# Three-pass products that walk the moved columns and their bank's columns from the last to the first

## What is computed

```python
def _swiglu(h, w13, w2):
    gte, up = jnp.split(h @ w13, 2, axis=-1)
    return (jax.nn.silu(gte) * up) @ w2

def peer_ffn(h, w_pq, sub_keys, expert_u, expert_v):
    ...
        u = jnp.take(expert_u, ic, axis=0)
        a = jnp.einsum('cd,chkd->chk', hc, u)
        w = gc * jax.nn.gelu(a, approximate=False)
        return jnp.einsum('chk,chkd->cd', w, jnp.take(expert_v, ic, axis=0))
```

## Time and profile before

| | us |
|---|---|
| median of 3 runs | 3823.09 |
| lowest and highest | 3820.19, 3826.91 |
| the profiled execution, its span | 3825.9 |
| TensorE busy in it | 3753.4 |
| VectorE, ScalarE, GpSimd busy | 2803.7, 1752.2, 576.4 |

### The profile page before, as it was taken

The page is one execution under the profiler, slowest core; times in us unless marked ns, Lnnn a source line. Parts: engine busy times, 40 slices in busy tenths (PEclk is TensorE's granted clock), DMA queues, the critical chain, the costliest instruction groups (busy, mean ns, idle before and its releaser), DMA issues.

```text
span 3825.9 us, 68450 instructions
## 1 busy us (share of the span) xinstructions
PE 3753.4 (98%) x22768; PEld 3354.5 (88%) x22768; DVE 2803.7 (73%) x4900; ACT 1752.2 (46%) x2723; POOL 576.4 (15%) x244
## 2 busy tenths in 40 slices
PE   8999999999999999999999999999999999999998
PEld 7888888888888879998999999888888999997886
DVE  7867777776863556654588888888644688888888
ACT  3223323223322354445546776333465557774334
POOL 0000000000000000055675000000356770000000
PEclk9999999999999999999999999999999999999999
DMA  6544434454542324563456666777634466666775
GB/s 252 177 158 156 158 132 153 145 181 138 176 138 85 97 67 153 181 209 117 142 180 224 208 206 202 241 242 240 228 126 145 155 228 207 209 212 220 241 241 197
DMA packets 203862, 685.43 MB, mean 179 GB/s; under 512 B 22560, under 2 KB 24864, under 8 KB 194336
## 3 DMA queue, kind: packets, MB, share of 16 engines
q1 hardware_dynamic: 174880, 573.45, 46.2%
q10 hardware_dynamic: 28800, 109.59, 7.8%
HBM read 646.25 MB, written 36.70 MB: 179 GB/s over the span
## 4 chain that ended last, share of the span: by engine, by line
PE 81%; POOL 8%; issue 7%; DVE 2%; DMA 1%; ACT 1%; POOLq 0%; SPq 0%; DVEq 0%; ACTq 0%
PE bank L584 25%; PE bank L586 25%; PE bank L585 25%; POOL low L544 8%; PE bank L1152 2%; PE bank L626 1%; PE bank L680 0%; PE bank L681 0%; PE bank L685 0%; PE bank L791 0%; DMA x<-in_x 0%; DVE low L1684 0%; PE bank L769 0%; PE bank L836 0%; DVE h L1663 0%
## 5 line engine op out<-in xcount | busy, mean ns | idle before, releaser
L1228 ACT ACTIVATE high<-raw 128x1024 fp32r<-128x1024 f32 x1044 | 1098.9, 1058 | 1288.8 <-PE bank L586 987.8
L584 PE MATMUL bank<-h_lo,high 128*128 128x256 f32 (+1 forms) x4080 | 1280.5, 314 | 7.0 <-ACT h_hi L1627 3.6
L586 PE MATMUL bank<-h_hi,low 128*128 128x256 f32 (+1 forms) x4080 | 1276.5, 313 | 0.0
L585 PE MATMUL bank<-h_hi,high 128*128 128x256 f32 (+1 forms) x4080 | 1274.4, 312 | 0.0
L1684 DVE TENSOR_TENSOR low<-raw,high 128x1024 fp32r<-128x1024 f32 x808 | 971.4, 1219 | 79.3 <-ACT high L1228 77.2
L544 POOL TENSOR_TENSOR low<-raw,high 128x1024 fp32r<-128x1024 f32 x240 | 576.2, 2407 | 2571.7 <-DVE low L1684 2325.3
L584 PEld LDWEIGHTS bank<-h_lo,high 128*128 128x128 f32 x4080 | 772.2, 189 | 56.6 <-DVE h_lo L1759 4.9
L585 PEld LDWEIGHTS bank<-h_hi,high 128*128 128x128 f32 x4080 | 772.2, 189 | 47.3 <-issue 0.7
L586 PEld LDWEIGHTS bank<-h_hi,low 128*128 128x128 f32 x4080 | 771.6, 189 | 46.5
L584 PE MATMUL bank<-low,weighed_hi 128*128 128x512 f32 x1024 | 401.1, 392 | 8.5 <-DVE weighed_lo L1684 8.5
L585 PE MATMUL bank<-high,weighed_hi 128*128 128x512 f32 x1024 | 400.7, 391 | 0.0
(11 more groups left out here) (319 smaller groups left out, 4825.6 us busy)
## 6 DMA issues: line engine op xcount, KB each, us to landing
raw<-in_experts SPq DMA_DIRECT2D x516, 512.0 KB, 3.5
raw<-in_w SPq DMA_DIRECT2D x176, 512.0 KB, 4.2
late_raw<-in_mod_late ACTq DMA_DIRECT2D x64, 1024.0 KB, 4.8
acts_spill<-acts_out ACTq DMA_DIRECT2D x128, 256.0 KB, 3.8
acts_in<-acts_spill SPq DMA_DIRECT2D x128, 256.0 KB, 3.4
raw<-in_w_in SPq DMA_DIRECT2D x56, 512.0 KB, 3.4
raw<-in_w SPq DMA_DIRECT2D x64, 384.0 KB, 3.1
raw<-in_w SPq DMA_DIRECT2D x64, 320.0 KB, 3.6
```

The costliest lines, as they stand in the source:

```text
L584: pe.matmul(out, a[0], b[1], start=start, stop=False, **more)
L585: pe.matmul(out, a[0], b[0], start=False, stop=False, **more)
L586: return pe.matmul(out, a[1], b[0], start=False, stop=stop, **more)
L1228: act.activation(high[:, slot * UNIT:(slot + 1) * UNIT], raw[:, slot * UNIT:(slot + 1) * UNIT], ACT.Copy)\
```

## The change

A helper `falling` reverses the columns of the views it is given. `product3` uses it for its bank and for both parts of the moved operand; the stationary operand is as before. `project_first` does the same for its own matmuls. Every matmul of these products thus reads its moved columns from the last to the first and writes the bank's columns from the last to the first, and each sum ends in the column where it was.

```diff
--- before.py
+++ after.py
@@ -579,8 +579,13 @@
                 pe.wait_ge(S["low_ready"], unit.next())
                 return [part[:, slot * UNIT:(slot + 1) * UNIT] for part in (high, low)]
 
+            def falling(*parts):
+
+                return [part[:, ::-1] for part in parts]
+
             def product3(out, a, b, start, stop, **more):
 
+                out, *b = falling(out, *b)
                 pe.matmul(out, a[0], b[1], start=start, stop=False, **more)
                 pe.matmul(out, a[0], b[0], start=False, stop=False, **more)
                 return pe.matmul(out, a[1], b[0], start=False, stop=stop, **more)
@@ -670,26 +675,26 @@
                 w = [take() for _ in outs]
 
                 def parts(n, k):
-                    return [part[:, k * P:(k + 1) * P] for part in w[n]], rhs[n](k)
-
+                    return [part[:, k * P:(k + 1) * P] for part in w[n]], falling(*rhs[n](k))
+
+                down = falling(*outs)
                 for k in range(KD // 2):
 
                     wait("normed", per_tile)
                     for n in range(len(outs)):
                         a, b = parts(n, k)
-                        pe.matmul(outs[n], a[0], b[0], start=(k == 0), stop=False)
-                        pe.matmul(outs[n], a[1], b[0], start=False, stop=False)
+                        pe.matmul(down[n], a[0], b[0], start=(k == 0), stop=False)
+                        pe.matmul(down[n], a[1], b[0], start=False, stop=False)
                     wait("split")
                     for n in range(len(outs)):
                         a, b = parts(n, k)
-                        pe.matmul(outs[n], a[0], b[1], start=False, stop=False)
+                        pe.matmul(down[n], a[0], b[1], start=False, stop=False)
                 T["normed"].next(per_tile * (KD - KD // 2))
                 for n in range(len(outs)):
                     for k in range(KD // 2, KD):
                         if n == 0:
                             wait("split")
-                        a, b = parts(n, k)
-                        mm = product3(outs[n], a, b, False, k == KD - 1)
+                        mm = product3(outs[n], [part[:, k * P:(k + 1) * P] for part in w[n]], rhs[n](k), False, k == KD - 1)
                     mm.then_inc(unit_used, 1)
 
             def up_tiles(n, cols, fresh=False):
```

## The result

The changed kernel takes 3877.31 us (median of 4 runs, 3870.59 to 3880.55) against 3824.11 for the kernel before beside it (4 runs, 3820.19 to 3826.91). The ratio is 1.0144, with a 95% interval of 1.0131 to 1.0156: slower by 1.4%, where 1.2% faster was forecast. All ratios are over fast executions alone; the single slow one of the runs told of here, 5331.8 us with all moved tiles 16 columns ahead, is in none of them.

The account below looks back on a forecast made before the run. The prediction took TensorE's matmul pace to bound the kernel; savings of 13.3, 29.4 and 1.9 us sum to 44.6, giving a span of 3781.3 and, with the profiled span 2.8 us over the median, 3779 us; range 3640 to 3965.

Parts of the forecast that it names:

- What bounds the kernel: Whole kernel: as long as its matmuls are apart, TensorE busy 98% of the span; 20,688 of 22,768 matmuls touched.
- The paces of before: Distances between starts: 226.7 ns aligned and 233.3 with h2 stationary at 512 columns; 120.0 aligned and 116.7 with h2 moved at 256.
- What I take: Three-pass products: walks starting apart and crossing sooner give every backward matmul the 10.0 ns excess of h2 moved at 256.
- The terms: Savings by matmul group: 13.3 us from aligned 256s, 29.4 and 1.9 from 512s, 0 elsewhere; sum 44.6 us.
- That all of it reaches the end: Other engines keep up, VectorE at 18.5 of 20 us, so all 44.6 us shorten the span to 3781.3.
- Slower by crossings: Rival: opposed walks meet three times as often, 6.6 ns on each of 20,496 matmuls, 135 us, 3958; chance 0.15.
- The indifferent case: Rival: direction doesn't matter because the excess is a fixed swap of weights; 3823 within 8 us; chance 0.20.
- A lost path: Rival: array reads or bank writes run at full rate only upwards, pace doubles, some 2956 us, 6779; chance 0.13.
- Most of the excess goes: Rival: all excess is meetings at the start and 512s never meet again; 183 us saved, 3640; chance 0.09.
- What would make it wrong: Closing signs: aligned and shifted paces not coming together; forecast short if one size gains and the other loses.

Follow-up runs that it names:

- AHEAD = 0: Kernel before, nothing reversed, with the 8 columns by which h2 is shifted taken away: 3835.5 us, one run, against 3819.5.
- The first pace measurement: Program of matmuls alone, 24 to a series, varying start and direction of moved operand and bank; at 512 columns 226.6 ns upwards, 233.3 with the moved operand downwards.

## Why the prediction was wrong

- **What bounds the kernel** held. TensorE's pace times the count of matmuls gave +57 us against 50 measured; the instructions and the chain's shares didn't move, and the clock went from 0.990 to 0.992.
- **The paces of before** The earlier trace rows held, and that a tile's start makes the difference was shown by AHEAD = 0. The mean of h2 was 117.2, not the 116.7 of the one stretch: 27 steps of one place are a sample, and the difference is 0.5 ns x 7488 = 4 us.
- **The step that failed is "What I take"**: that a backward walk, since it starts apart from the other, has the 10.0 ns excess of the earlier trace rows, at 512 columns as at 256. It has two errors. The first is the generalisation. The 116.7 at 256 columns was the only evidence that a start ahead helps, and it was carried to 512. The first pace measurement shows the opposite there: 233.3 at 8 ahead, 233.05 at 8 behind, 226.6 at 0. The earlier trace rows was read as "a start behind costs"; what holds at 512 is that any start costs which isn't the same up to a multiple of 64 columns. This makes the 29.4 us expected of the 512s +58.9 instead, 88 us of the 94 between the span forecast (3781.3) and the one measured (3875.5). The second is the geometry. That a backward walk begins at the far end of its tile and crosses the other one doesn't matter: with blocks of 64 falling it does both and takes 226.7. The order inside each 64 columns does: 233.3 with each 64 reversed in its place.
- **The terms.** 8832 of 512: -3.3 ns each expected, +6.67 measured. 3984 of 256: -3.33 expected, -1.6 measured. 7488 with h2 moved: 0 expected, +0.64. 192 with h2 stationary: -10.0 expected, 0 measured. 192 of 128 columns: 0 and 0 (their stage waited 4 us less).
- **That all of it reaches the end** held; some 8 us of the loss by the means were taken up by waits that became shorter, 4.2 of them in the key scores.
- **The rivals.** Slower by crossings, at 3958, named the sign, the pace to look for (233 and more) and the price of 6.6 ns, which was right to 0.1 ns. It was charged to every matmul of both widths, 20,496, and falls on 8832. Its mechanism, meetings on the way, isn't supported: at 512 columns neither fewer stationary columns (233.3 downwards at 128 to 32) nor another path across the tile with the same order inside each 64 (233.3) changed the downward pace. The indifferent case holds for the bank, and in sum for the 256s (0.9998), where -6.4 and +4.8 us happen to cancel, and not for the 512s. What spoke for it, the same 13.3 ns at 256 and 512 columns as of a fixed cost, doesn't hold between them: 12.0 ns at 288, 16.6 at 480. A lost path is excluded by the bank's 226.7 and the moved operand's 233.3. Most of the excess goes: the least seen with any moved walk, one column, is 218.7, so only 8.0 of the 13.3 ns are seen to hang on where the moved reads go.
- **What would make it wrong** was named in its last clause, one width gaining and the other losing. That clause should have had a case of its own: with the two widths priced apart, each by its own rows, the 512s had one row for a start that isn't the same, and it was slower.
- **The range**, 3640 to 3965, holds the 3877 by luck. It reaches that far for slower by crossings alone, whose mechanism isn't supported and which charged both widths; no case of the prediction puts the time where it was measured.

**What stays open.** Why the order of reads inside 256 bytes changes the pace, and why the difference of the two starts does; why the sign of both differs between 256 and 512 columns; and what sets the two levels of one walk. No run here turns the walk over the stationary columns; that wasn't tried.

## What to carry to other kernels

When the moved operand can be walked in any order, keep it rising within each 64 columns of four bytes wherever a matmul has 384 or more of them, and at 512 start it at the same place inside 64 columns as the stationary operand; the order of such stretches, and the bank's direction, were free here. A pace that depends on alignment belongs to one width: read it from rows of the width that has the most matmuls before using it there, and measure it alone if there are none, because a few ns in 9000 matmuls were the whole result. A quicker start found in a loop of matmuls alone is a candidate and no gain: of the 3.4 ns that 16 columns ahead gained on 8 there, 0.9 was left in the kernel.

## What the runs showed of the hardware

- A matmul of 512 columns takes 226.7 ns where the starts of both operands differ by nothing or by a multiple of 64 columns (256 bytes), 228.7 to 236.8 with other starts (233 for most, on either side), and 233.3 to 236.7 walked downwards. At 256 columns it is 120.0 upwards and aligned, and from 113.3 to 126.3 otherwise.
- Shifting the stationary operand alone has the effect of shifting the moved one the other way: 233.3 against 233.05 for 8 columns, 229.0 against 228.9 for 48.
- Backwards inside blocks of 16 is much worse than all the way backwards: 266.7 against 233.3, and 133.3 against 118.4. Inside blocks of 4 it is free.
- Reading one column over and over still takes 218.7 ns for 512 steps and 112.0 for 256, so 5.3 ns of the excess stay even where the moved operand never goes on to another column.
- Thirty-two stationary columns in place of 128 made the upward pace at 512 columns slower, 231.6 against 226.6, and at 256 columns quicker, 113.3 against 119.7.
- One walk can have two paces, each held for 30 steps and more: 113.4 and 117.8 at 256 columns, 16 ahead.
